# The MLP of a hybrid decoder layer as 2x2 block products: seven products in place of eight, with the weight sums on GpSimd

## What is computed

```python
    hm = _rms(x, norm_mlp) @ w_up                      # 544x2048 @ 2048x8192
    x = x + jnp.square(jax.nn.relu(hm)) @ w_down       # 544x8192 @ 8192x2048
...
y = _rms(x, norm_final)
```

## Time and profile before

| | us |
|---|---|
| median of three runs | 2851.53 (2851.3 to 2851.89) |
| profiled execution, span | 2850.1 |
| TensorE busy | 2811.6 |
| start of the `o_proj_1` stretch in the chain | 1192.77 |
| last matmul of the MLP | 2834.28 |
| from there to the end of the span | 15.8 |

### The profile page before, as it was taken

The page is one execution under the profiler, slowest core; times in us unless marked ns, Lnnn a source line. Parts: engine busy times, 40 slices in busy tenths (PEclk is TensorE's granted clock), DMA queues, the critical chain, the costliest instruction groups (busy, mean ns, idle before and its releaser), DMA issues.

```text
span 2850.1 us, 52719 instructions
## 1 busy us (share of the span) xinstructions
PE 2811.6 (99%) x21932; PEld 2750.2 (96%) x21932; DVE 1181.6 (41%) x1523; ACT 695.7 (24%) x817; POOL 54.7 (2%) x98
## 2 busy tenths in 40 slices
PE   8999999999999999999999999999999999999997
PEld 8989999999999969699999999999999999999997
DVE  7656434334542243454333333333333333333357
ACT  6532211112321221232212112122121121221233
POOL 1100000000000010000000000000000000000000
PEclk9999999999999999999999999999999999999999
DMA  8763222232234354422222222222222222222244
GB/s 270 226 192 108 90 85 86 88 88 90 87 113 170 95 213 166 163 88 83 89 89 89 87 84 87 89 88 88 85 84 88 88 88 88 84 86 88 89 131 153
DMA packets 85701, 316.54 MB, mean 111 GB/s; under 512 B 9696, under 2 KB 13920, under 8 KB 81536
## 3 DMA queue, kind: packets, MB, share of 16 engines
q1 hardware_dynamic: 76160, 265.68, 30.0%
q0 software_dynamic: 9472, 49.85, 4.8%
HBM read 306.22 MB, written 9.28 MB: 111 GB/s over the span
## 4 chain that ended last, share of the span: by engine, by line
PE 97%; DMA 2%; DVE 1%; issue 0%; SPq 0%; ACT 0%; POOL 0%; DVEq 0%
PE psum_main L1047 91%; PE psum_main L1154 3%; DMA cache_ring_a<-cache_v 1%; PE psum_main L1331 1%; PE psum_side L1227 1%; PE psum_main L1262 0%; PE psum_side L1303 0%; DMA mem_raw<-mem_t 0%; PE psum_side L1314 0%; DVE y_out L1015 0%; PE psum_side L1047 0%; PE psum_side L1103 0%; DVE temp L620 0%; DVE unit_low L600 0%; SPq L286 0%
## 5 line engine op out<-in xcount | busy, mean ns | idle before, releaser
L1047 PE MATMUL psum_main<-inner_a,unit_high 128*128 128x272 f32 x7680 | 1283.8, 288 | 0.0
L1047 PEld LDWEIGHTS psum_main<-inner_a,unit_high 128*128 128x128 f32 x7680 | 1087.0, 188 | 3.6 <-issue 3.4
L412 ACT ACTIVATE unit_high<-unit_raw 128x1024 fp32r<-128x1024 f32 x498 | 527.6, 1060 | 1904.9 <-PE psum_main L1047 1850.6
L1047 PE MATMUL psum_main<-inner_b,unit_high 128*128 128x272 f32 x5664 | 957.2, 288 | 0.9 <-DVE inner_b L988 0.9
L600 DVE TENSOR_TENSOR unit_low<-unit_raw,unit_high 128x1024 fp32r<-128x1024 f32 x498 | 609.0, 1224 | 520.4 <-ACT unit_high L412 517.1
L1047 PEld LDWEIGHTS psum_main<-inner_b,unit_high 128*128 128x128 f32 x5664 | 809.5, 188 | 1.9 <-DVE inner_b L988 1.1
L1047 PE MATMUL psum_main<-inner_a,unit_low 128*128 128x272 f32 x3840 | 792.6, 287 | 0.0
L1047 PE MATMUL psum_main<-inner_b,unit_low 128*128 128x272 f32 x2832 | 605.6, 287 | 0.0
L1047 PEld LDWEIGHTS psum_main<-inner_a,unit_low 128*128 128x128 f32 x3840 | 599.3, 188 | 0.0
L1047 PEld LDWEIGHTS psum_main<-inner_b,unit_low 128*128 128x128 f32 x2832 | 450.2, 188 | 0.0
L775 DVE TENSOR_TENSOR residual<-psum_main,residual 128x544 f32 x176 | 127.6, 725 | 624.3 <-PE psum_main L1047 624.3
(11 more groups left out here) (131 smaller groups left out, 787.9 us busy)
## 6 DMA issues: line engine op xcount, KB each, us to landing
unit_raw<-weights SPq DMA_DIRECT2D x498, 512.0 KB, 3.6
cache_ring_a<-cache_v POOLq DMA_DIRECT2D x16, 1024.0 KB, 6.8
cache_ring_t<-cache_k POOLq DMA_DIRECT2D x8, 1024.0 KB, 7.9
cache_ring_a<-cache_k POOLq DMA_DIRECT2D x8, 1024.0 KB, 7.0
residual<-x_t POOLq DMA_DIRECT2D x8, 544.0 KB, 5.6
y_t<-y_out POOLq DMA_DIRECT2D x4, 544.0 KB, 3.5
y_t<-y_out SPq DMA_DIRECT2D x8, 272.0 KB, 2.2
k_t<-temp POOLq DMA_DIRECT2D x16, 128.0 KB, 4.3
```

The costliest lines, as they stand in the source:

```text
L412: act.activation(WHI[:, s, :], RAW[:, s, :], ACT.Copy).then_inc(high_ready, 1)
L1047: ins = pe.matmul(out, weights_at(w), moving, start=first and n == 0, stop=last and n == len(passes) - 1)
```

## The change

The MLP's matrices are cut into 2x2 blocks. The tokens form two halves (272 each), the contracted dimension two halves, the output rows two halves. The eight block products of such a multiplication are replaced by seven, made of sums of blocks (the Winograd form of Strassen's method).

- **Quads.** The work is 64 "quads": 32 for up (2 output tiles each), 32 for down (4 output tiles each). A quad has four weight blocks w11, w12, w21, w22, each 128x1024, and seven products of 24 matmuls (128x272); a product goes to one bank or, in down, to two banks in turn of 12. Products 0, 2, 4 and 6 accumulate in one chain of PSUM, so each waits until ACT or DVE has read the state before it (`act_read`, `dve_read`, `down_read`).
- **Weight sums.** Products 2 to 5 need sums of the weight blocks. GpSimd makes them, four additions of 128x1024 per quad, in the order 1, 3, 2, 4, in place in `RAW` and in a fifth buffer `SUMW`, into which w22 is loaded a second time. ACT and DVE split the seven weight operands (`high`, `low`).
- **Token sums.** `o_proj_1` no longer rounds tiles to `A`. When it has ended, the norm factor is computed, `X` is scaled in place (16 tiles), four of the seven token operands are made by sums, and all seven are split into `X7`. `X` is before that stored to DRAM by GpSimd and comes back when down begins.
- **Inner layer.** All of up runs first. Its result (ReLU, square, four tiles of 272 per quad) is mixed into seven operands, split, staged in `STAGE` and stored in DRAM (1.95 MB per quad). Down loads the seven operands of a chunk (1.11 MB each) into the room of the token operands, two chunks at a time, refilled during a chunk's last quad.
- **End.** The last down is no longer halved; squares, norm factor and all 16 output tiles follow the last product, and SP stores them.

The programs are written out without loops for the 64 quads. The diff, cut to its core:

```diff
-    ("o_proj_1", 16, 16, 16, 0, 0, 16, 16),
+    ("o_proj_1", 16, 16, 0, 0, 0, 0, 16),
...
+QUADS = 32
+PRODUCTS = 7
+SLOT_OF = (0, 1, 2, 3, 0, 1, 2)
+FREED_BY = (3, 3, 3, 7, 4, 4, 4)
+SOURCE_OF = (0, 1, 0, 4, 2, 1, 3)
+SUM_OF = {2: 3, 3: 1, 4: 2, 5: 4}
+STAGED_AT = (0, 1, 3, 4, 5, 2, 6)
+HK = CH // 2
...
+        B7 = [[at(f"hidden_{z}_{i}", [P, HK, 2, HALF], F32R,
+                  slots_at[(PRODUCTS * z + i) // 2] + (PRODUCTS * z + i) % 2 * HK * 2 * HALF * 4)
+               for i in range(PRODUCTS)] for z in range(2)]
+        SUMW = at("unit_sum", [P, UNIT], F32, misc_at)
...
+            for q in range(2 * QUADS):
...
+                    sp.wait_ge(h_ready, KT)
+                    sp.dma_start(into(q, SUMW[:, :]), w22).then_inc(mlp_raw[4], 16)
+                else:
+                    sp.wait_ge(mlp_ready, PRODUCTS * (q - 1) + 4)
+                    sp.dma_start(into(q, SUMW[:, :]), w22).then_inc(mlp_raw[4], 16)
+                    sp.wait_ge(mlp_ready, PRODUCTS * (q - 1) + 5)
+                    sp.dma_start(into(q, RAW[:, 2, :]), w21).then_inc(mlp_raw[2], 16)
+                    sp.wait_ge(mlp_sum, 4 * q)
+                    sp.dma_start(into(q, RAW[:, 0, :]), w11).then_inc(mlp_raw[0], 16)
+                    sp.wait_ge(mlp_ready, PRODUCTS * (q - 1) + 6)
+                    sp.dma_start(into(q, RAW[:, 1, :]), w12).then_inc(mlp_raw[1], 16)
+                    sp.wait_ge(mlp_ready, PRODUCTS * q)
+                    sp.dma_start(into(q, RAW[:, 3, :]), w22).then_inc(mlp_raw[3], 16)
...
+            for n in range(KT // 2):
+                pool.wait_ge(psum_free, START["o_proj_1"]["tiles"] + 2 * n + 2)
+                pool.dma_start(two_tiles(n), X[:, 2 * n:2 * n + 2, :]).then_inc(x_spilled, 16)
...
+            def store_hidden(q):
+                pool.wait_ge(stage_ready, 2 * q + 2)
+                pool.dma_start(hidden7[q // HK, :, q % HK], STAGE[:, :, :, :].bitcast(F32)).then_inc(hid_stored, 16)
+            def load_hidden(c, i):
+                pool.dma_start(B7[c % 2][i][:, :, :, :].bitcast(F32).rearrange("p j s n -> p (j s) n"),
+                               hidden7[c, :, :, :, STAGED_AT[i], :].rearrange("p j s n -> p (j s) n")) \
+                    .then_inc(hid_loaded[c % 2][i], 16)
...
+            def sum_1(q):
+                pool.wait_ge(mlp_raw[2], 16 * (q + 1))
+                pool.wait_ge(mlp_raw[4], 16 * (q + 1))
+                pool.tensor_tensor(SUMW[:, :], SUMW[:, :], RAW[:, 2, :], ALU.add).then_inc(mlp_sum, 1)
...
+            def sum_3(q):
+                pool.wait_ge(mlp_raw[0], 16 * (q + 1))
+                pool.wait_ge(mlp_sum, 4 * q + 1)
+                pool.tensor_tensor(RAW[:, 2, :], RAW[:, 2, :], RAW[:, 0, :], ALU.add).then_inc(mlp_sum, 1)
...
+            def sum_2(q):
+                pool.wait_ge(mlp_sum, 4 * q + 2)
+                pool.wait_ge(mlp_ready, PRODUCTS * q + 1)
+                pool.tensor_tensor(RAW[:, 0, :], RAW[:, 0, :], SUMW[:, :], ALU.add).then_inc(mlp_sum, 1)
...
+            def sum_4(q):
+                pool.wait_ge(mlp_sum, 4 * q + 3)
+                pool.wait_ge(mlp_ready, PRODUCTS * q + 2)
+                pool.tensor_tensor(RAW[:, 1, :], RAW[:, 1, :], RAW[:, 0, :], ALU.add).then_inc(mlp_sum, 1)
...
+            for q in range(2 * QUADS):
+                sum_2(q)
+                c = (q - QUADS - 3) // 4 + 2
+                refill = q >= QUADS and q % 4 == 3 and c < FF_CHUNKS
+                if refill:
+                    pool.wait_ge(mlp_used, PRODUCTS * q + 1)
+                    load_hidden(c, 0)
+                if q == QUADS - 1:
+                    pool.wait_ge(hid_stored, 16 * HK)
+                    pool.wait_ge(mlp_used, last + 1)
+                    load_hidden(0, 0)
+                    load_hidden(0, 1)
+                if q == QUADS:
+                    pool.wait_ge(dve_read, 3 * QUADS)
+                    pool.dma_start(X[:, 0:3, :], x_kept[0:3].rearrange("t p n -> p t n")).then_inc(x_back[0], 16)
+                    pool.wait_ge(hid_ready, QUADS)
+                    pool.dma_start(X[:, 3:5, :], x_kept[3:5].rearrange("t p n -> p t n")).then_inc(x_back[1], 16)
+                sum_4(q)
+                if q == QUADS - 1:
+                    for i in range(2, PRODUCTS):
+                        pool.wait_ge(mlp_used, last + i // 2 + 1)
+                        load_hidden(0, i)
+                if refill:
+                    for i in range(1, 5):
+                        pool.wait_ge(mlp_used, PRODUCTS * q + i + 1)
+                        load_hidden(c, i)
+                if 1 <= q <= QUADS:
+                    store_hidden(q - 1)
+                if q == QUADS:
+                    pool.wait_ge(hid_stored, 16 * QUADS)
+                    pool.dma_start(X[:, 5:KT, :], x_kept[5:KT].rearrange("t p n -> p t n")).then_inc(x_back[2], 16)
+                    for i in range(PRODUCTS):
+                        pool.wait_ge(mlp_used, last + (PRODUCTS + i) // 2 + 1)
+                        load_hidden(1, i)
+                if q + 1 < 2 * QUADS:
+                    sum_1(q + 1)
+                if refill:
+                    pool.wait_ge(mlp_used, PRODUCTS * q + 6)
+                    load_hidden(c, 5)
+                if q + 1 < 2 * QUADS:
+                    sum_3(q + 1)
+                if refill:
+                    pool.wait_ge(mlp_used, PRODUCTS * q + 7)
+                    load_hidden(c, 6)
...
+                if tail:
+                    act.wait_ge(mlp_used, PRODUCTS * q)
+                    act.activation(RELU[:, 1, :], chain(n), ACT.Relu, scale=-1.0).then_inc(act_read, 1)
+                    rectify(n, 3, 3, 1.0)
...
+                if tail:
+                    if n:
+                        act.wait_ge(stage_ready, 2 * n)
+                    act.wait_ge(relu_done, 3 * n + 3)
+                    act.wait_ge(act_read, 4 * n + 4)
+                    act.activation(HID[:, :, :], RELU[:, :, :], ACT.Square).then_inc(hid_ready, 1)
...
+                if tail:
+                    if n:
+                        act.wait_ge(hid_stored, 16 * n)
+                    act.activation(STAGE[:, 0, 0:3, :], HID[:, 0:3, :], ACT.Copy).then_inc(stage_high, 1)
...
+            def normalise_tile(t):
+                dve.scalar_tensor_tensor(X[:, t, :], X[:, t, :], PAR[:, G_MLP + t:G_MLP + t + 1], RSTD[:, :],
+                                         ALU.mult, ALU.mult).then_inc(h_ready, 1)
...
+            for g in range(2):
+                for k in range(4 * g, 4 * g + 4):
+                    normalise_tile(k)
+                    normalise_tile(CH + k)
+                if g:
+                    low_tokens(0, 0, 1, b_block(0, 0, 0))
+                    low_tokens(1, 0, 2, b_block(1, 0, 0))
+            low_tokens(0, 1, 3, b_block(0, 0, 1))
+            low_tokens(1, 1, 4, b_block(1, 0, 1))
+            for g in range(2):
+                k = slice(4 * g, 4 * g + 4)
+                t2, t3, t4 = (X7RAW[i][:, k, 1, :] for i in (2, 4, 6))
+                dve.wait_ge(h_ready, KT)
+                dve.tensor_tensor(t3, b_block(1, 1, g), b_block(0, 1, g), ALU.subtract).then_inc(tok_raw, 1)
+                dve.wait_ge(tok_raw, 3 * g + 1)
...
+            def read_up(q, i, n, bank, partial, count_act, sign):
+                dve.wait_ge(mlp_used, PRODUCTS * q + i + 1)
+                dve.wait_ge(act_read, 4 * q + count_act)
+                if q:
+                    dve.wait_ge(hid_ready, q)
+                dve.tensor_tensor(RELU[:, n, :], bank, partial, ALU.add).then_inc(dve_read, 1)
...
+            for q in range(2 * QUADS + 1):
+                n, ahead, up, down_q = q - 1, q < 2 * QUADS, q < QUADS, QUADS <= q < 2 * QUADS
+                tail = 1 <= q <= QUADS
+                if q > QUADS:
+                    add_down(q - 1, 6, 1, 0, chain(q - 1), ALU.subtract)
+                if ahead:
+                    low(q, 2)
+                if down_q:
+                    add_down(q, 0, 0, 0, chain(q), ALU.add)
+                if ahead:
+                    low(q, 3)
+                if up:
+                    read_up(q, 1, 0, S[:, 0, 0:HALF], UP_P1[:, :], 1, 1)
+                if ahead:
+                    low(q, 4)
+                if down_q:
+                    add_down(q, 1, 0, 0, b2, ALU.add)
+                if tail:
+                    mix_hidden(n)
+                if down_q:
+                    add_down(q, 2, 0, 1, chain(q), ALU.add)
+                if ahead:
+                    low(q, 5)
+                if tail:
+                    low_hidden(n, 0)
+                if down_q:
+                    add_down(q, 3, 1, 1, b3, ALU.subtract)
+                if ahead:
+                    low(q, 6)
+                if tail:
+                    low_hidden(n, 1)
+                if up:
+                    read_up(q, 4, 2, chain(q), UP_P5[:, :], 3, 1)
+                if down_q:
+                    add_down(q, 4, 1, 1, chain(q), ALU.subtract)
+                if q + 1 < 2 * QUADS:
```

(45 more changed lines are left out.)

426 lines of the change are left out of this document (297 added, 129 removed).

## The result

| | before | changed |
|---|---|---|
| median | 2851.68 us (2851.3 to 2851.89) | 2920.58 us (2917.11 to 2923.38) |
| profiled span | 2850.1 us | 2919.6 us |

The ratio is 1.0242, with a 95% interval of 1.0228 to 1.0257. The change costs 69 us, where the forecast had it gain 27.

A forecast was written before the change was run, and what follows sets the result against it. TensorE, busy 2811.6 of 2850.1 us, was taken to bound the kernel. 1289.2 + 1350.0 + 53.5 + 38 + 36 + 30 + 26 = 2822.7, median 1.4 above: 2824 us (chance 0.37, own range 2795 to 2860); whole range 2755 to 2912.

The forecast's parts named there:

- start: Start of the MLP after `o_proj_1`: TensorE idle 48.5 us, and 5 more for the first sums in DVE's list.
- up: The 32 up quads: interference of GpSimd's sums with DVE costs 1.2 us a quad, 38 us.
- passage: From up to down: idle of 20 and 14 us with late first operands, 36 us, ends 25 and 60.
- down: Down quads: refill waits and late weights, 30 us taken, between 12 without interference and 60.
- end: Behind the last product: squares, norm factor, 16 outputs, a store and handovers, 26 us.
- I take 1.2, just over the best packing: Cost per up quad if GpSimd and DVE can't run at once, from a range of 0 to 2.1 us.
- They take turns: Rival, chance 0.32: sums and DVE passes exclude each other by whole instructions; up 77, down 60, total 2899 us.
- My t: Time of one GpSimd addition of 128x1024, in no row of the trace: taken as 2.3 us.
- The ring: Up's loop of GpSimd's sums, ACT's and DVE's passes and the store's issue: 12.45 + 3t = 19.4 us, under TensorE's 21.1.
- Weights come late: Down: refill and weight loads exceed 311 GB/s in 21.1 us; 0.4 us a quad counted without interference, 12 us.
- The second wait, 14 us: Second down quad, product 2: GpSimd's store, eight loads, sums and two splits take 35.4 us, due after 21.1.
- The first, 20 us for the addition that needs `X`: First down quad, product 2: waits for `X`, behind 13.2 MB of loads and stores, 42.5 us at 311 GB/s.

The follow-up runs named there:

- e5: Changed kernel with each GpSimd sum replaced by three memsets in a row, held about as long but reading nothing, sums left out: 2781.4 us.
- e1: Changed kernel with the four weight sums of every quad on VectorE instead of GpSimd, everything computed: 2798.53 us, ratio to the kernel before 0.9812.
- bare: No run but a reference row: the quads at 21.05 us each, as they run without a stall; 631.5 us for down quads 34 to 63.
- e7: e1 with the loads of the stored inner layer spread over the four quads before each piece: 2753.72 us, ratio to the kernel before 0.9655.
- e9: Changed kernel, sums still on GpSimd, with only the loads of the stored inner layer spread over four quads: 2917.42 us.
- e3: Changed kernel with each GpSimd sum replaced by one memset of the tile it writes, sums left out: 2767.6 us.
- e2: Changed kernel with each GpSimd sum replaced by a multiply-add with constants over one tile, other summand left out: 2792.2 us.

## Why the prediction was wrong

By its own terms, against the profiled execution of 2919.6 us:

| term | predicted | measured |
|---|---|---|
| to the end of `o_proj_1` | 1289.2 | 1287.0 |
| matmuls of the MLP | 1350.0 | 1347.3 |
| start | 53.5 | 56.2 |
| up | 38 | 81.7 |
| passage | 36 | 41.3 |
| down | 30 | 75.9 |
| end | 26 | 30.2 |

TensorE's saving came in full; two terms carry 90 of the 97 us missed.

**Up.** The step that failed is "I take 1.2, just over the best packing": it cost 2.4 us a quad, and 2.8 with the clock. The mechanism was named, in the rival "They take turns", which had an up quad at 23.5 us, and the quads came out at 23.45. Its signs are all there: splits grown from 1.22 to 2.42 us, sums of 3 us and more, ACT standing 109.3 us of the up stretch for sum 2, with DVE behind it. My t was right: the shortest sum took 2.33 us, where 2.3 was taken. The estimate of 2.25 from the Trainium skill (GPSIMD Engine Reference, Performance versus the Vector engine) is near it too. The best packing of 21.8 us would need splits and sums to find each other's gaps; but the order on each engine is fixed, the sums come in a block right behind the store, and DVE's splits of the next quad are due just then. That the rival's 23.5 came so near is luck: it is made of 14.0 + 9.2 us of work one after another, but DVE's reads of PSUM do not wait for a sum, and DVE stands idle for 5.86 us of the quad. What sets its length is the ring.

**The ring**, whose sum was to be 19.4 us with 1.7 to spare, failed by two terms. From the split of 1605.12 to the same split of the next quad at 1628.58 are 23.46 us: 12.95 to the store's issue (10.63 in my list, and in it now 1.2 of the split's waiting for its turn and 0.51 and 0.87 us of DVE standing for ACT, less a little overlap), 0.59 for the issue, 3.11 and 3.28 for sums 1 and 3 with their turns, 2.43 for sum 2, and 1.10 for ACT, each with its handover. DVE's waiting for ACT within the ring was not in the list; in e5 it is 0.37 and 0.87 us, and e5 came 1.0 above 20.3. So the ring decided from about t = 2.5, not from 2.9, and the 1.5 us that turns put on sums 1 and 3 and the 1.2 on the split went straight into the quad. I had priced ring and turns apart; they stand in the same loop and add.

**The clock** had no term. In 8 of the 29 quads from 2 to 30 the granted clock is at the lower of its two levels (1.2 GHz of 2.4) for 3.4 us, each time after the idle before product 2, and such a quad takes 24.9 us. Two neighbours, by windows:

```profile
1933.80:1958.70 24.90, 22.72 (x171) 22.53 (x170) 14.79 (x16) 12.28 (x17) 11.55 (x6) 0.93 0.50 183
1958.70:1982.10 23.40, 21.22 (x170) 21.03 (x169) 14.79 (x16) 12.29 (x17) 11.46 (x6) 1.00 0.53 196
```

That is 8 x 1.5 = 12 of the 81.7 us; the idle itself is 68.1. In e1 and e5 the clock stays up throughout these quads. The other stages have the same cost: at the lower level the matmuls start 227 ns apart and not 125.6, and so do some 39 in quads 0 and 1, 61 in the passage and 137 in down, which makes about 4, 6 and 14 us. With the 12 in up, the clock is over a third of the 97 us missed.

**Down.** Both prices failed, mine of 30 and the turns' of 60. "Weights come late" was in the text, with 0.4 us a quad; one burst costs some 6 us even without turns (e1: 43.9 over bare in down, and 2.9 once it is spread), and with them the weight loads beside it took up to 19 us, where the earlier trace rows had 3.6. From e1, e7 and e9: the sums on DVE alone are worth 32.0 us in down, the spread alone -2.8, both together 73.0. The two don't add up, so a sum by terms could not have found them one by one. Nor is e1 a measure of the turns alone: e3 and e5 keep the burst and have sums on neither engine, and their down takes 649 us, 26 less than e1's. What these 26 us are is not shown.

**Passage.** 36 was right to 5 us, in part by luck, as one place was wrong. The second wait, 14 us at product 2 of the second down quad, came as worked out, and its chain is the one predicted, with 16.8 us:

```profile
2131.61 8.27 DMA hidden_kept<-hidden_staged
...
2140.45 1.09 POOL residual L577
2141.54 3.12 POOL hidden L519 x4
...
2145.07 2.63 POOL hidden L519 x3
2147.71 2.36 POOL unit_sum L527
...
2150.21 2.33 POOL unit_raw L532
...
2152.62 2.35 POOL unit_raw L537
2154.99 1.07 ACT unit_high L769
```

The first, 20 us for the addition that needs `X`, did not: 4.0, 6.6 and 2.0 us instead, in quads 31 and 32, the 6.6 behind a weight load of 16.68 us that lay beside the loads of the inner layer. These 12.6 us, a wait of 5.7 before quad 34 and some 6 of the lower clock stand in the place of the 20.

**Start and end.** 56.2 for 53.5: four of DVE's token passes lay beside the first sums and took 3.3 to 3.4 us instead of 1.2 to 1.3, so 8 us where I put 5. At the end the 8 matmuls that sum the squares took 2.95 us against the 0.9 taken from two, and from the last output pass to the end of the span are 5.0 us, where 3.2 stood for store and handovers.

**The chances.** The turns had 0.32 against 0.37 of the forecast, and the trace before showed nothing of them. Nothing showed their absence either, and the Trainium skill (SBUF — State Buffer, Who interferes with whom) named exactly the two instructions that this change lays beside each other; the splits of 2.42 us agree with it. And that rival's own 2899 was 22 us short, 16 of them in the down stage.

## What to carry to other kernels

Elementwise work on GpSimd with SBUF inputs is not beside DVE's two-input work but takes turns with it: add up both engines' passes as one engine (here 12.6 + 9.2 = 21.8 us against 21.1, so they don't fit), then ask whether DVE alone would do the sum faster (here 1.22 us against 2.33, and the whole change turned from 69 us lost to 53 gained). When a loop of engines handing buffers round is within a microsecond or two of the period, list the waits of every member in it, and put all costs that fall into it into one sum. Test a repair on the kernel whose ring has room: the same spread of loads was worth 44.8 us there and nothing on the full one.

## What the runs showed of the hardware

- The lock between the two engines holds for a GpSimd instruction with one SBUF input too (e2: 1.05 us alone, 1.90 at L537 behind a DVE pass with two SBUF inputs), and not for a memset (955 and 957 ns, splits 1222 and 1224). DVE's reads of PSUM, which have one input in SBUF, don't wait: 0.43 to 0.44 us for L1312, also in the 31 of 96 that start while a sum runs. ACT's splits neither: 1057 ns at L769, 1060 in the earlier trace rows.
- Where TensorE stood 2.35 us in every quad, the granted clock was at the lower level for 3.4 us in 8 of 29 quads; with no idle (e1) in none of them. A stall cost more than its length.
- 512 KB loads of one queue landed in 3.8 to 4.3 us at the median in the changed kernel and its variants, and in 12.5 to 19.0 (changed kernel, 2300 to 2340 us) while another queue brought 1 MB pieces back to back.
